# Where the last two thirds of a conditioning product are computed: TensorE beside attention, or VectorE beside the input projection

## The chip, the cores and the metric

One Trainium2 chip, one of its cores. The metric is the device time of one execution in microseconds (us), median of three runs. The core has five engines with instruction streams of their own: TensorE (PE in the profile; its weight loads are PEld), VectorE (DVE), ScalarE (ACT), GpSimd (POOL) and SyncE (SP), which here only issues transfers. They wait for each other through semaphores.

## The reference

A transformer step for 512 prompt tokens and 64 sample tokens (T = 576, model width D = 1024). What matters here:

```
mod = silu(c) @ w_ada + b_ada                    # c: 2 x 1024, w_ada: 1024 x 6144
sh1, sc1, gt1, sh2, sc2, gt2 = split(mod, 6)
h   = x * (1 + sc1) + sh1
z   = h @ w_in                                   # 1024 x 2112, in 17 blocks of 128 columns
cq, ckv = rms_norm(z[first 6 blocks]), rms_norm(z[next 2 blocks])
...   q = cq @ w_uq, attention over 4 heads, a gated branch, mix @ w_o
x1  = LN(alpha * x + (1 + gt1) * mix)            # gt1 needed here
h2  = x1 * (1 + sc2) + sh2                       # sc2, sh2 here
x2  = LN(alpha * x1 + (1 + gt2) * PEER(h2))      # gt2 at the very end
```

Only sh1 and sc1 are needed before the input projection. PEER, the mixture of 16384 small experts, takes the last three quarters of the time and is not touched.

## The kernel before

All activations lie transposed, channels on the 128 partitions and 576 tokens along the free axis in two halves of 288. Dense float32 products are made of three matmuls in a rounded format: `w_hi*x_hi`, `w_hi*x_lo`, `w_lo*x_hi`. For each block of 128 output columns SyncE loads 512 KB of weights into one of four slots of `w_raw` (function `stream`), ScalarE copies them to `w_hi`, then VectorE (`linear`, L1169) or GpSimd (`low_parts`, L428) subtracts to get `w_lo`; `w_hi` and `w_lo` have two buffers each. TensorE runs 48 matmuls a block, and ScalarE copies the result out of PSUM into `z` (function `out`). ScalarE's program for block b is: the high part of block b, then the copying out of block b-1.

The input projection is `w_in` (blocks 0 to 7, the low-rank q and kv) and `w_in2` (blocks 8 to 16). In `w_in` VectorE makes the low parts and, behind them, the squares of each block (`low_rank_squares`, L1188); in `w_in2` GpSimd makes the low parts. After block 8 TensorE sums the squares over the partitions with a matrix of ones (`low_rank_sums`, semaphore `rowsA`); VectorE scales the sums (L1192, L1193), ScalarE takes the roots, VectorE inverts (L1195), scales q and kv (L1198, L1202).

The product `silu(c) @ w_ada` is done on TensorE with silu(c) as the stationary operand (128 x 2) and the weights as the moving one. A "row" of `ada` is 512 KB and two matmuls of 512 columns, each of which the trace shows as two instructions. Sixteen rows give sh1 and sc1 before the projection. The other 32 rows come later: `ada2` (16 rows, one in each of the first 16 of the 20 units of attention, after `scores` and before `turned`), `ada3` (8, after attention, while the norm of the mixed heads is computed) and `ada4` (8, while LN1 is computed). A unit is one head and one tile of queries: scores, maximum (VectorE), exponential (ScalarE), norm (VectorE), transpose (TensorE, `turned`, L686), copy (ScalarE), product with the values (`values`). `new_keys` transposes a tile of new keys for output; its first one stands before the first unit, with a wait for ScalarE's copy behind it.

SyncE's queue holds the weight loads in program order; a load waits until its slot's previous block has its low part.

## Time and profile before

| | us |
|---|---|
| median of 3 runs | 2003.26 (1999.28 to 2005.17) |
| the profiled execution, own time | 2004.94 |
| its span in the profile | 2003.1 |
| granted TensorE clock, mean | 0.978 of full |

| engine | busy us | share |
|---|---|---|
| TensorE | 1912.8 | 95% |
| VectorE | 1399.2 | 70% |
| ScalarE | 744.3 | 37% |
| GpSimd | 422.1 | 21% |

Stages, from the same profile: conditioning and entry norm until 65 us, input projection 65 to 183, `w_uq`, keys and values until 257, attention 257 to 348, norm and `w_o` until 437, LN1 until 486, `w_pq` and PEER after that. The span includes all of it; a share of busy time is an average over these stages, so a change to one of them is read in its own window.

### The profile page before, as it was taken

Reading aid. Unit: us, or ns where it says so; the run is one execution under the profiler, and the core shown is the slowest. Engines: PE = TensorE matmul, PEld = TensorE weight load, DVE = VectorE, ACT = ScalarE, POOL = GpSimd, SP = SyncE. Lnnn points to the kernel's source line nnn. Section 1 sums busy time; section 2 is a strip of 40 time slices with the busy share of each in tenths; the row PEclk is TensorE's granted clock in tenths of the full one; section 3 lists DMA queues with packets and bytes.
Section 4 is the critical chain, followed back from the end, with each engine's and each line's share of the span. In section 5 each row is a group of like instructions: output and inputs, shape, how many; then the busy total and the mean of one; then the engine's idle time right before and its main releaser. Section 6 shows DMA issues by size and latency. Waiting matters only on the chain.

```text
span 2003.1 us, 27471 instructions
## 1 busy us (share of the span) xinstructions
PE 1912.8 (95%) x10275; PEld 1688.0 (84%) x10275; DVE 1399.2 (70%) x2739; ACT 744.3 (37%) x1154; POOL 422.1 (21%) x338
## 2 busy tenths in 40 slices
PE   7799999897998999999999999999999999999995
PEld 1799744685997999999999999989999999999995
DVE  3542444636887788987987998766767777777776
ACT  1223244212122333664565466623333333333332
POOL 1124100203320112221221222241222212122212
PEclk9899989998998999999999999999999999999997
DMA  8112123314223677887788788899999999999971
GB/s 282 64 64 89 43 80 107 127 43 137 66 71 107 213 217 225 296 291 255 258 298 273 238 300 297 313 370 340 319 311 311 319 313 322 311 316 313 313 246 69
DMA packets 189728, 447.16 MB, mean 223 GB/s; under 512 B 15792, under 2 KB 105920, under 8 KB 185888
## 3 DMA queue, kind: packets, MB, share of 16 engines
q1 hardware_dynamic: 150752, 304.13, 46.3%
q0 software_dynamic: 38848, 141.34, 20.1%
q8 instruction: 78, 1.28, 0.2%
q14 instruction: 50, 0.41, 0.1%
HBM read 383.46 MB, written 61.95 MB: 222 GB/s over the span
## 4 chain that ended last, share of the span: by engine, by line
PE 89%; DVE 6%; DMA 2%; ACT 1%; issue 1%; SPq 1%; POOL 1%; POOLq 0%; ACTq 0%; DVEq 0%
PE ps L492 88%; DMA w_raw<-peer_v 1%; SPq L378 1%; DMA gath<-peer_u,expert 0%; DMA consts_sb<-consts 0%; DVE tmp L1149 0%; PE ps L686 0%; DVE h2T L1149 0%; DVE rows L1310 0%; DVE x0T L1352 0%; DMA w_raw<-ada 0%; DVE stats L1576 0%; POOL act_lo L435 0%; DVE x0T L1351 0%; DVE x0T L1127 0%
## 5 line engine op out<-in xcount | busy, mean ns | idle before, releaser
L492 PE MATMUL ps<-act_hi,w_hi 128*128 128x448 f32 (+1 forms) x1752 | 603.1, 344 | 26.6 <-DVE act_lo L1158 11.9
L857 ACT ACTIVATE w_hi<-w_raw 128x1024 fp32r<-128x1024 f32 (+1 forms) x303 | 319.3, 1054 | 811.4 <-PE ps L492 798.8
L492 PE MATMUL ps<-act_hi,w_lo 128*128 128x448 f32 (+1 forms) x1752 | 592.8, 338 | 0.0
L492 PE MATMUL ps<-act_lo,w_hi 128*128 128x448 f32 (+1 forms) x1752 | 592.8, 338 | 0.0
L1396 DVE TENSOR_TENSOR w_lo<-w_raw,w_hi 128x1024 fp32r<-128x1024 f32 x256 | 313.6, 1225 | 282.4 <-ACT w_hi L857 282.0
L492 PE MATMUL ps<-ga_hi,w_hi 128*128 128x448 f32 x1024 | 374.7, 366 | 4.4 <-DVE ga_lo L1512 4.4
L492 PE MATMUL ps<-ga_hi,w_lo 128*128 128x448 f32 x1024 | 374.6, 366 | 0.0
L492 PE MATMUL ps<-ga_lo,w_hi 128*128 128x448 f32 x1024 | 374.6, 366 | 0.0
L492 PEld LDWEIGHTS ps<-act_hi,w_hi 128*128 128x128 f32 x1752 | 333.6, 190 | 43.6 <-issue 16.0
L492 PEld LDWEIGHTS ps<-act_hi,w_lo 128*128 128x128 f32 x1752 | 333.0, 190 | 15.6
L492 PEld LDWEIGHTS ps<-act_lo,w_hi 128*128 128x128 f32 x1752 | 333.5, 190 | 14.7
L480 POOL DMA_INDIRECT gath<-peer_u,expert x128 | 164.3, 1283 | 577.0 <-DVE act_v L1517 484.3
L480 POOL DMA_INDIRECT gath<-peer_v,expert x128 | 127.0, 992 | 476.1 <-DVE f_tok L1525 461.3
L492 PEld LDWEIGHTS ps<-ga_hi,w_hi 128*128 128x128 f32 x1024 | 192.7, 188 | 20.0 <-DVE w_lo L1396 4.7
L492 PEld LDWEIGHTS ps<-ga_lo,w_hi 128*128 128x128 f32 x1024 | 192.8, 188 | 15.3
L492 PEld LDWEIGHTS ps<-ga_hi,w_lo 128*128 128x128 f32 x1024 | 192.7, 188 | 15.3
L1525 DVE SCALAR_TENSOR_TENSOR f_tok<-gath,act_g,f_tok 128x1024 f32<-128x1024 f32 x128 | 163.5, 1278 | 0.5
L1517 DVE CUSTOM_DVE_ANT_0 gath<-gath,h_tok 128x1024 f32<-128x1024 f32 x128 | 154.2, 1219 | 10.8 <-DMA gath<-peer_u,expert 10.8
L428 POOL TENSOR_TENSOR w_lo<-w_raw,w_hi 128x1024 fp32r<-128x1024 f32 (+1 forms) x33 | 77.1, 2338 | 218.8 <-ACT w_hi L857 218.7
L857 ACT ACTIVATE piece<-ps 128x512 f32<-128x512 f32 x112 | 112.4, 1109 | 0.0
L492 PEld LDWEIGHTS ps<-one_i,one_j 128*128 128x128 f32 x896 | 108.8, 192 | 1.5
L492 PE MATMUL ps<-one_i,one_j 128*128 128x128 f32 x896 | 109.1, 275 | 0.0
(220 smaller groups left out, 1692.0 us busy)
## 6 DMA issues: line engine op xcount, KB each, us to landing
w_raw<-peer_uT SPq DMA_DIRECT2D x128, 512.0 KB, 4.6
w_raw<-peer_v SPq DMA_DIRECT2D x128, 512.0 KB, 5.4
early_activations<-e_out SPq DMA_DIRECT2D x128, 224.0 KB, 5.2
dense_gates<-piece SPq DMA_DIRECT2D x28, 1024.0 KB, 6.8
a_in<-early_activations SPq DMA_DIRECT2D x128, 224.0 KB, 5.7
g_in<-dense_gates SPq DMA_DIRECT2D x64, 448.0 KB, 6.7
w_raw<-ada SPq DMA_DIRECT2D x48, 512.0 KB, 3.3
w_raw<-w_in SPq DMA_DIRECT2D x17, 512.0 KB, 3.2
```

What stands on the lines that cost most here:

```text
L378: sp.dma_start(g_in[:, k % 2, sub].rearrange("p s i t -> p s (i t)"), src).then_inc(s_gi[k % 2], 16)
L428: nc.gpsimd.tensor_tensor(w_lo[:, g, 0:kk * P], w_raw[:, slot, 0:kk * P], w_hi[:, g, 0:kk * P].bitcast(F32), ALU.subtract).then_inc(s["wlo ...
L480: pool.indirect_dma_start(out=gath[:, n % GB, :], out_offset=None, in_=table, in_offset=bass.IndirectOffsetOnAxis(ap=expert[:, k:k + 1], a ...
L492: return nc.tensor.matmul(out, lhsT, rhs, start=start, stop=stop)
L857: return nc.scalar.activation(out, in_, func, **kw)
L1396: v.tensor_tensor(LO[c % 3], w_raw[:, (R0 + c) % RING], HI[c % 3].bitcast(F32), ALU.subtract).then_inc(s["wlo"], 1)
L1517: v.tensor_tensor_reduce(gath[:, n % GB], gath[:, n % GB], h2_tok[:], 1.0, 0.0, ALU.mult, ALU.add, act_v[:, n:n + 1]).then_inc(s["gd"], 1)
L1525: v.scalar_tensor_tensor(f_tok[:], gath[:, n % GB], act_g[:, k:k + 1], f_tok[:], ALU.mult, ALU.add).then_inc(s["gd"], 1)
```

## The change

The 32 later rows leave TensorE. Their weights are stored the other way round (`ada_rows`: 32 rows of 128 outputs x 1024 inputs, 512 KB each as before), and VectorE computes each as two dot products along the free axis with silu(c), which is laid out on all partitions (`silu_row`, 1 MB, a broadcast load on GpSimd's queue, then one activation). Twenty-two rows are computed during `w_in` and the first of `w_in2`, ten after the scaling of q and kv. In exchange GpSimd makes the low parts of all 17 blocks but the first too (VectorE made those of blocks 1 to 7), and ScalarE makes the squares of blocks 0 to 7, each just ahead of its copy out of PSUM. ScalarE's root of the sums stands one block later (`at={3: ...}`). The rows go through three buffers (`ada_in`), loaded by SyncE between the weight blocks; the load of row n waits until n-2 rows are computed. Attention keeps `new_keys` alone, spread over units 1, 3, 6, 8 and 11.

```diff
+NEW_AT = (1, 3, 6, 8, 11)
-ORDER = dict(ada=2 * KD, w_in=Z_KR, w_in2=Z_N - Z_KR, w_uq=6, ada2=2 * KD, ada3=KD, w_o=KD, ada4=KD, w_pq=HP)
+ORDER = dict(ada=2 * KD, w_in=Z_KR, w_in2=Z_N - Z_KR, w_uq=6, w_o=KD, w_pq=HP)
+ROWBUF = 3
+ROW_LOADS = (3, 2, 3, 2, 3, 2, 3, 2, 3, 2, 3, 2, 2)
+EARLY_ROWS = 22
...
+            def load_row(n):
+                wait(sp, s["adar"], n - ROWBUF + 1)
+                sp.dma_start(ada_in[:, n % ROWBUF], a["ada_rows"][n]).then_inc(s_ar[n % ROWBUF], 16)
...
+            for name in ("w_in", "w_in2"):
+                load = stream(name, a["w_in"][FIRST[name]:])
+                for b in range(ORDER[name]):
+                    load(b, b % RING)
+                    step_at = FIRST[name] + b - RING + 1
+                    if step_at >= 0:
+                        for n in range(rows_at, min(NROW, rows_at + (ROW_LOADS + (0, 0))[step_at])):
+                            load_row(n)
...
+            pool.dma_start(silu_row[:].rearrange("p c k -> p (c k)"), a["c_row"].partition_broadcast(P)).then_inc(s_cr, 16)
             pool.dma_start(ckvT[:, :, SEQ:NEW], a["cacheT"]).then_inc(s_cache, 16)
...
+            low_parts("w_in", 1)
             low_parts("w_in2")
...
-            new_keys(0)
-            pe.wait_ge(s["ote"], 1)
             for i, (h, t) in enumerate(units):
                 if i + 2 < len(units):
                     scores(i + 2)
-                if i % 4 == 0 and 0 < i <= ORDER["ada2"]:
-                    ada_columns(first + i // 4 - 1, ps[:, 6, 2 * i - 8:2 * i])
-                if i < ORDER["ada2"]:
-                    ada_row(first + i // 4, i % 4)
-                else:
-                    new_keys(i - ORDER["ada2"] + 1)
+                if i in NEW_AT:
+                    new_keys(NEW_AT.index(i))
...
-            for g in range(2):
-                ada_rows(ADA_AT["ada3"] // 4 + g)
...
-            for g in range(2):
-                ada_rows(ADA_AT["ada4"] // 4 + g)
...
+                        f(tmp[:, b, :].rearrange("p (s h) -> p s h", s=2), ps[:, pair:pair + 2, 0:H], ACT.Square).then_inc(s["sqz"], 1)
...
-            linear("w_in2", z[:, Z_KR:], at={2: low_rank_deviations}, then="w_uq")
+            linear("w_in2", z[:, Z_KR:], at={3: low_rank_deviations}, then="w_uq")
...
+            def mod_row(n):
+                if n == 0:
+                    dve.wait_ge(s["silur"], 1)
+                wait(dve, s["adar"], n)
+                dve.wait_ge(s_ar[n % ROWBUF], 16 * (n // ROWBUF + 1))
+                for c, out in ((0, ada_scratch[:]), (1, ada_in[:, n % ROWBUF])):
+                    ins = v.tensor_tensor_reduce(out, ada_in[:, n % ROWBUF], silu_row[:, c], 1.0, 0.0, ALU.mult, ALU.add,
+                                                 mod[:, 2 * KD + n, c:c + 1])
+                ins.then_inc(s["adar"], 1)
+
+            for n in range(EARLY_ROWS):
+                mod_row(n)
...
+            for n in range(EARLY_ROWS, NROW):
+                mod_row(n)
+            dve.wait_ge(s["adar"], NROW)
+            conditioning(2 * KD, 6 * KD)
```

How the instructions stand. First SyncE's queue in the input projection, where `w_raw<-w_in` is the load of one weight block. Before, the 17 loads follow each other:

```order
L352 DMA w_raw<-w_in 128x1024 x17
L352 DMA w_raw<-w_uq 128x768 x6
```

Of the change, from block 11's load on (`ada_in<-ada_rows` is the load of rows to be dotted; the first three rows here are rows 20 to 22):

```order
L369 DMA ada_in<-ada_rows 128x1024 x3
L363 DMA w_raw<-w_in 128x1024
L369 DMA ada_in<-ada_rows 128x1024 x2
L363 DMA w_raw<-w_in 128x1024
L369 DMA ada_in<-ada_rows 128x1024 x3
L363 DMA w_raw<-w_in 128x1024
L369 DMA ada_in<-ada_rows 128x1024 x2
```

What moved: the three weight loads here are those of blocks 12, 13 and 14, and block 14's now stands behind the loads of rows 25, 26 and 27, each of which waits for a computed row.

Second VectorE at the place where the sums of squares are taken up. Before:

```order
L1169 TENSOR_TENSOR w_lo<-w_raw,w_hi 128x1024
L1188 TENSOR_TENSOR tmp<-z 128x576 x2
L1192 TENSOR_SCALAR rows<-ps 128x576
L1193 TENSOR_SCALAR rows<-ps 128x576
L1195 RECIPROCAL rows<-rows 128x1152
L1198 SCALAR_TENSOR_TENSOR tmp<-z,vecs_sb,rows 128x576 x6
```

Of the change (an `ISA` row with `ada_in` as input is one dot product, the `mod 128x1` row behind it writes its sum):

```order
L1206 ISA ada_scratch,mod<-ada_in,silu_row 128x1024 [waits ada_row_landed0,s_adar]
L1206 ISA mod 128x1
L1206 ISA ada_in,mod<-ada_in,silu_row 128x1024
L1206 ISA mod 128x1
L1215 TENSOR_SCALAR rows<-ps 128x576 [waits s_rowsA,s_lo_odd,s_hlo]
L1216 TENSOR_SCALAR rows<-ps 128x576
L1218 RECIPROCAL rows<-rows 128x1152 [waits s_std]
```

What moved: in place of seven low parts and eight squares, 44 dot products now stand between the projection's start and L1215, and 20 more behind the scaling of kv.

## Rows read from the trace of the kernel before

**Rows 1.** The page, engines over the span and the chain that ended last

```profile
PE 1912.8 (95%) x10275; PEld 1688.0 (84%) x10275; DVE 1399.2 (70%) x2739; ACT 744.3 (37%) x1154; POOL 422.1 (21%) x338
PE 89%; DVE 6%; DMA 2%; ACT 1%; issue 1%; SPq 1%; POOL 1%; POOLq 0%; ACTq 0%; DVEq 0%
```

**Rows 2.** Windows: length; PE, PEld, DVE, ACT, POOL busy; clock, DMA share, GB/s

```profile
65.00:183.00 118.00, 118.00 (x848) 116.10 (x848) 34.88 (x31) 28.56 (x35) 26.22 (x13) 0.98 0.23 80
...
340.00:348.00 8.00, 5.52 (x36) 3.66 (x34) 2.90 (x12) 4.43 (x14) 2.73 (x6) 1.00 0.13 42
...
357.00:370.00 13.00, 12.32 (x33) 2.61 (x32) 11.62 (x7) 3.10 (x4) 0.68 (x1) 1.00 0.63 205
...
455.00:470.00 15.00, 13.47 (x35) 2.63 (x33) 14.68 (x20) 3.81 (x6) 2.38 (x2) 1.00 0.73 220
```

**Rows 3.** Window of one head of attention (five units), same columns

```profile
301.00:322.60 21.60, 21.50 (x88) 8.80 (x87) 8.86 (x34) 8.92 (x27) 0.00 (x0) 1.00 0.35 123
```

**Rows 4.** The same window, ScalarE's instructions on prob alone (the exponentials)

```profile
301.00:322.60 21.60, 5.30 (x18) 1.00 0.35 123
```

**Rows 5.** Timeline of TensorE: four rows of ada3 (start, us, engine, line, operation)

```profile
356.70 7.03 PE L492 MATMUL ps<-w_raw,silu_c 128*2 128x512 f32 x16
```

**Rows 6.** Timeline: GpSimd's low part, ready ahead of w_o's first matmul

```profile
374.59 2.85 POOL L428 TENSOR_TENSOR w_lo<-w_raw,w_hi 128x1024 fp32r<-128x1024 f32 x1
...
377.55 0.58 PE L492 MATMUL ps<-act_hi,w_hi 128*128 128x288 f32 x1 [3.93 <-issue]
```

**Rows 7.** Timeline of VectorE: dot products of 1024 elements back to back

```profile
1343.08 1.22 DVE L1517 CUSTOM_DVE_ANT_0 gath<-gath,h_tok 128x1024 f32<-128x1024 f32 x1
...
1344.22 1.22 DVE L1517 CUSTOM_DVE_ANT_0 gath<-gath,h_tok 128x1024 f32<-128x1024 f32 x1
1345.37 0.08 DVE L1517 DVE_READ_ACCUMULATOR2_ANT act_v<- 128x1 f32 x1
```

**Rows 8.** Line 1217 on VectorE, ns min/median/max of its four

```profile
L1217 DVE TENSOR_TENSOR tmp<-z x4: 743/751/2404, 194.6 to 198.2; 128x576 f32<-128x576 f32 x4
```

**Rows 9.** Timeline of VectorE and GpSimd at that place

```profile
194.56 4.42 DVE L1217 TENSOR_TENSOR tmp<-z 128x576 f32<-128x576 f32 x4
194.82 2.21 POOL L428 TENSOR_TENSOR w_lo<-w_raw,w_hi 128x768 fp32r<-128x768 f32 x1 [2.91 <-ACT w_hi L857]
```

**Rows 10.** Timeline of VectorE in the input projection

```profile
63.99 3.98 DVE L1158 TENSOR_TENSOR act_lo<-tmp,act_hi 128x576 fp32r<-128x576 f32 x4
...
132.18 0.76 DVE L1192 TENSOR_SCALAR rows<-ps 128x576 f32<-128x576 f32 x1 [12.68 <-PE ps L492]
...
146.86 3.94 DVE L1202 SCALAR_TENSOR_TENSOR ckvT<-z,vecs_sb,rows 128x512 f32<-128x512 f32 x4
```

**Rows 11.** Timeline of ScalarE and GpSimd around blocks 12 to 14

```profile
157.61 0.65 ACT L857 ACTIVATE z<-ps 128x576 f32<-128x576 f32 x1 [4.76 <-PE ps L492]
158.16 1.05 ACT L857 ACTIVATE w_hi<-w_raw 128x1024 fp32r<-128x1024 f32 x1
163.97 0.65 ACT L857 ACTIVATE z<-ps 128x576 f32<-128x576 f32 x1 [4.76 <-PE ps L492]
...
159.35 2.40 POOL L428 TENSOR_TENSOR w_lo<-w_raw,w_hi 128x1024 fp32r<-128x1024 f32 x1 [3.96 <-ACT w_hi L857]
```

**Rows 12.** The page, DMA issues: KB each, median us to landing

```profile
w_raw<-w_in SPq DMA_DIRECT2D x17, 512.0 KB, 3.2
```

**Rows 13.** Windows of 2 us at the projection's start, columns as in rows 2

```profile
66.00:68.00 2.00, 2.00 (x10) 2.00 (x10) 2.00 (x3) 0.00 (x0) 0.68 (x1) 0.50 0.00 0
68.00:70.00 2.00, 2.00 (x12) 2.00 (x11) 1.10 (x1) 0.00 (x0) 0.00 (x0) 0.67 0.00 0
...
74.00:76.00 2.00, 2.00 (x18) 2.00 (x17) 1.52 (x2) 1.13 (x2) 0.00 (x0) 1.00 0.00 0
```

**Rows 14.** The first 20 us: a piece of the chain, and the window

```profile
14.68 7.20 DMA w_raw<-ada
...
0.00:20.00 20.00, 8.90 (x16) 1.48 (x16) 6.19 (x13) 1.64 (x3) 5.38 (x13) 1.00 0.90 313
```

More of the change, by code:

```diff
@@ L127 @@
 S0 = SPLIT_AT["w_pq"] + HP
-FIRST = dict(ada=0, ada2=3 * KD, ada3=2 * KD, ada4=5 * KD, w_in=0, w_in2=Z_KR)
-ADA_AT = dict(ada=0, ada2=2 * KD, ada3=4 * KD, ada4=5 * KD)
-WIDTH = dict(ada=KD, ada2=KD, ada3=KD, ada4=KD, w_in=KD, w_in2=KD, w_uq=QK, w_o=KD, w_pq=KD)
+FIRST = dict(w_in=0, w_in2=Z_KR)
+NROW = 4 * KD
+ROWBUF = 3
+ROW_LOADS = (3, 2, 3, 2, 3, 2, 3, 2, 3, 2, 3, 2, 2)
+EARLY_ROWS = 22
+WIDTH = dict(ada=KD, w_in=KD, w_in2=KD, w_uq=QK, w_o=KD, w_pq=KD)
 def wait(eng, sem, value):
@@ L213, in build @@
         r_T = at("r_T", [P, KD, T], R["z"])
+        silu_row = at("silu_row", [P, 2, D], R["q"])
+        ada_in = at("ada_in", [P, ROWBUF, D], R["q"] + 8192)
+        ada_scratch = at("ada_scratch", [P, D], R["q"] + 8192 + ROWBUF * 4096)
+        assert R["q"] + 12288 + ROWBUF * 4096 <= R["kr"]
         h2T = at("h2T", [P, KD, T], R["z"] + KD * T * 4)
@@ L348, in load @@
                     if held.startswith("ada"):
-                        wait(sp, s["adaused"], b + (g0 - RING - RING_AT[held] + ADA_AT[held] + 1))
+                        wait(sp, s["adaused"], b + (g0 - RING - RING_AT[held] + 1))
                     else:
@@ L352, in load @@
                     sp.dma_start(w_raw[:, slot, 0:width], dram[b]).then_inc(s_w[slot], 16)
-                in_steps(sp, ORDER[name], RING, load)
-            for name in ORDER:
-                stream(name, a[name.rstrip("234")][FIRST[name]:] if name in FIRST else a[name])
+                return load
+            def load_row(n):
+                wait(sp, s["adar"], n - ROWBUF + 1)
+                sp.dma_start(ada_in[:, n % ROWBUF], a["ada_rows"][n]).then_inc(s_ar[n % ROWBUF], 16)
+            in_steps(sp, ORDER["ada"], RING, stream("ada", a["ada"]))
+            rows_at = 0
+            for name in ("w_in", "w_in2"):
[6 more added lines that the diff above has]
+                            load_row(n)
+                        rows_at += ROW_LOADS[step_at] if step_at < len(ROW_LOADS) else 0
+            for n in range(rows_at, NROW):
+                load_row(n)
+            for name in ("w_uq", "w_o", "w_pq"):
+                in_steps(sp, ORDER[name], RING, stream(name, a[name]))
             def load_block(c):
@@ L495, in ada_row @@
             def ada_row(g, j):
[L497 to L498 removed]
+                r = 4 * g + j
                 if j == 0:
@@ L702, in _ @@
             pe.wait_ge(s["vte"], NT)
-            first = ORDER["ada"] // 4
             scores(0)
@@ L911, in out @@
                     func = ACT.Gelu_apprx_tanh if name == "w_in2" and b > 0 else ACT.Copy
-                    f(to.rearrange("p (s h) -> p s h", s=2), ps[:, pair:pair + 2, 0:H], func).then_inc(s["evac"], 1)
-                in_steps(act, ORDER[name], RING, one)
+                    if name == "w_in":
+                        if b == 0:
+                            act.wait_ge(s["hlo"], KD // 2)
+                            act.wait_ge(s["lo_odd"], ODD["cq"])
+                        f(tmp[:, b, :].rearrange("p (s h) -> p s h", s=2), ps[:, pair:pair + 2, 0:H], ACT.Square).then_inc(s["sqz"], 1)
+                    f(to.rearrange("p (s h) -> p s h", s=2), ps[:, pair:pair + 2, 0:H], func).then_inc(s["evac"], 1)
+                if name == "w_in":
+                    for b in range(ORDER[name]):
+                        one(b, b % RING)
+                else:
+                    in_steps(act, ORDER[name], RING, one)
                 if callable(then):
@@ L987, in _ @@
                 ins.then_inc(s["pte"], 1)
-                if i % 4 == 0 and 0 < i <= ORDER["ada2"]:
-                    ada_copy(ORDER["ada"] // 4 + i // 4 - 1)
                 if 2 <= i < 2 + GH:
                     gated_squares(i - 2)
-                if i > ORDER["ada2"]:
-                    new_keys(i - ORDER["ada2"])
                 if i >= NT + 2 and (i - 2) % NT == 0:
                     head_squares((i - 2) // NT - 1)
-            new_keys(NT - 1)
             head_squares(HEADS - 1)
@@ L1000, in _ @@
             f(rows[:, 0:2], rows[:, 0:2], ACT.Sqrt).then_inc(s["std"], 1)
-            ada_copy(ADA_AT["ada3"] // 4)
             act.wait_ge(s["nv"], 16)
@@ L1006, in _ @@
                 if k == 3:
-                    ada_copy(ADA_AT["ada3"] // 4 + 1)
                     first_high("w_o")
@@ L1181, in row @@
                 return rows[:, i].rearrange("p (s h) -> p s h", s=2)
[L1183 to L1189 removed]
+            def mod_row(n):
[9 more added lines that the diff above has]
+                mod_row(n)
+            dve.wait_ge(s["hlo"], KD // 2)
+            dve.wait_ge(s["lo_odd"], ODD["cq"])
             dve.wait_ge(s["rowsA"], 1)
```

47 lines of the change are left out of this document (16 added, 31 removed).

## The prediction

> **What bounds the kernel now.** I read the page first: TensorE is busy 95% of the span and holds 89% of the chain that ended last [rows 1]. The change touches only the first 490 us, so the average says little; next come the windows by stage, and the question in each is whether TensorE waits. In the input projection it does not: 118.00 busy us in 118 [rows 2], while VectorE works 34.88 and GpSimd 26.22. In attention one head takes 21.60 us, of which TensorE is busy 21.50 [rows 3]: there too TensorE is the bound. In the two windows that hold `ada3` and `ada4` it is busy as well (12.32 of 13, 13.47 of 15), but beside it VectorE is busy 11.62 and 14.68 with a reciprocal and with LN1 [rows 2], and those are what the next product waits for. So the change takes work from TensorE where TensorE is the bound (attention) and where it is not (the two norms), and adds work to VectorE where VectorE has slack. What has to be read is whether the slack is there when it is wanted.
>
> **Removed: `ada2`.** Four rows one behind the other take 7.03 us [rows 5], 1.76 a row. A head of five units carries five, 8.8 us; TensorE alone would need 21.5 - 8.8 = 12.7 us a head. Then another loop binds, in which each step waits for the one before: exponential (ScalarE), norm, copy and next maximum (all VectorE). Its work in the window is ScalarE's 5.30 [rows 4] and VectorE's 8.86 [rows 3], 14.2 us; with some 20 hand-overs and two or three places where ScalarE's copy or square is longer than VectorE's maximum I take 16.3. Saved: 5.3 us a head, and the rows lie in 16 of 20 units, 3.2 heads: **17.0 us**. Ends: 13 (TensorE's own order holds up two units of each head) and 20.
>
> **Removed: `ada3`, `ada4`.** Worth nothing. `w_o`'s first matmul, at 377.55, follows GpSimd's low part, which ran from 374.59 to 377.44 [rows 6], and this hangs on the heads' norm, not on TensorE. `ada4` ends before LN1 does [rows 2]. Bounds: 0 to 1 us gained (ScalarE loses four small copies). Both products start at half clock today after idle time and will again.
>
> **Added at the start: the broadcast.** 1 MB is put on GpSimd's queue ahead of the cached keys. DMA is at 90%, 313 GB/s, in the first 20 us, and TensorE's chain waits 7.20 us for an `ada` load there [rows 14]. At 313 GB/s, 1 MB is 3.3 us; the load shares rather than queues behind it. Between 0 and 3.3 I take **+2.0**. The activation over 2048 elements on ScalarE falls into idle time while VectorE fills `tmp`.
>
> **Moved in the input projection.** This is the large term. I follow one path.
>
> First the port. Of four equal element-wise operations at L1217 three took 0.75 us and one 2.404 [rows 8]; GpSimd's low part ran from 194.82 to 197.03 [rows 9], and the long one is exactly the remainder of that plus its own 0.75. So an operation of VectorE with two inputs in SBUF stood still while GpSimd subtracted. The dot products have two inputs in SBUF as well; no row shows one beside a GpSimd operation. I take them to stand still too, for 2.40 us a block [rows 11]; the other end is that they run on.
> The Trainium skill, "SBUF — State Buffer", section "Who interferes with whom", says that a VectorE instruction with two SBUF inputs and a GpSimd instruction that reads SBUF exclude each other for the whole instruction. By that rule the dots are blocked; by plain sharing of the time the stage would lose less, as in the first rival.
>
> A row of two dots: 1343.08 to 1345.45 is 2.37 [rows 7], with a semaphore 2.42. VectorE starts on them when `act_lo` is done, 67.97 [rows 10]; now GpSimd's low part of block 1 comes in between, 70.4. TensorE's first block waits for the same `act_lo`, which I keep in the sum by measuring from 70.4. Twenty-two rows are 53.2 us, and the low parts of about ten blocks fall among them, 24.0: done at 147.6. The sums of squares were taken up at 132.18 [rows 10], so they are now 15.4 late. From there to the end of the scaling it took until 150.80 [rows 10], 18.6 us; again 18.6 gives 166.2. (ScalarE sits in front of the root meanwhile, and TensorE's block 12 comes some 4 us late; this is swallowed by what follows.)
>
> Then SyncE. Block 14's load stands behind the load of row 27, which waits for 25 rows computed: three more, 7.3 us, so 173.5. The load lands 3.2 later [rows 12], 176.7; high part 1.05, a dot in flight about 0.6, low part 2.40 [rows 11]: TensorE starts block 14 at 180.8. Before, block 13's result was fetched at 163.97 [rows 11], so block 14 started there: **16.8 us late**. Blocks 15 and 16 come just in time behind it. After such a gap TensorE restarts at half clock: 10 matmuls in 2 us against 18 [rows 13]; at the projection's start this lasted until about 69.3, some 4.4 us from its first matmul, a loss of **1.9**. Sum of the stage: **+18.7**.
>
> What is queued behind: ScalarE's copies out wait behind the high part; VectorE's last rows end near 198, before TensorE ends the stage (183 + 18.7), so `w_uq` isn't held up further. GpSimd's low part takes twice VectorE's time, but it is ready before the block ends: copy and square 1.3, high part 1.05, wait at most 1.2, low part 2.40, together 6.0 of a block of 6.36 (163.97 - 157.61, rows 11). Moving squares and low parts therefore costs nothing by itself; without that cover it is the third rival. `low_rank_squares` on VectorE was never on the path.
> Ends of this term: 10.1 if the dots are not blocked (below), 23 if each row costs 2.6.
>
> **Sum.** 2004.94 (profiled execution, own time) + 18.7 + 2.0 - 17.0 = 2008.6, that is +3.7; on the median of 2003.26, which lies 1.7 below the profiled one, **2007**. Two large terms of opposite sign nearly cancel. What this kernel's measurement can tell from no change is about 0.3%, 6 us.
>
> **Rivals.**
> (1) *The dots run beside GpSimd.* For: nothing in the trace shows this operation blocked. Against: [rows 8, 9]. Then 22 rows end near 122, before the sums; the root waits for ScalarE's new place behind block 11 and is some 7.5 us later than now, the scaling ends at 158, block 14's load goes at 165.4, TensorE starts it at 172.2: 8.2 + 1.9 = 10.1 for the stage. 2007 - 8.6 = 1998, from there to 1994 if attention gives 20.
> (2) *TensorE's clock stays low in attention (slower).* With 12.7 us of work in 16.3 TensorE is busy 78%. At half clock its 12.7 become nearly 25, and attention is then no shorter than today's 21.6. Against: in 340 to 348, units that already carry no `ada`, it was busy 5.52 of 8 us and the clock stayed at 1.00 [rows 2]. It decides if the half clock, which attention starts with, lasts for more than a head and a half; lost half of the time it leaves 5 of the 17 us: 2019.
> The Trainium skill, "TensorE: Matmul & The Clock Gate", section "HAM oscillation — how this bites in real kernels", tells of a kernel whose waits between tiles throttle the clock again each time. By that rule the gaps of a unit would have to be long; here they are 1 to 2 us, so the trace and the rule leave this a small chance.
> (3) *GpSimd's low parts are late in every block.* If a request waits for both dots of a row, 2.3 us, the low part is ready after 7.05 us of 6.36, 0.7 us a block over 15 blocks: some 10 us before the big gap, part of it swallowed: 2013 to 2019. It decides from a wait of 1.6 us on.
>
> **Chances.** Forecast (stage +14 to +23, attention -14 to -19, total 2001 to 2013) 0.58; rival (1) 0.22; (2) 0.12; (3) 0.08. Within 0.3% is 1997.3 to 2009.3: of the forecast two thirds, of (1) 0.6, of (3) little: 0.50. Faster by more: a third of (1) and a tail of the forecast where attention gives 20 and the broadcast nothing, together 0.15. Slower: a third of the forecast's lower gains, (2) and (3): 0.35. The forecast's own range is 2001 to 2013; the range that leaves out no more than 2 in 10 is 1996 to 2018.
>
> **What the new profile would show.** Right: a gap of TensorE of 10 us or more ahead of block 14, with SyncE's load of it behind `ada_in` loads; dots of which some last 3.6 us instead of 1.2, those beside a GpSimd low part; sums taken up on VectorE near 147; a head of attention in 16 to 17 us at clock 1.00; no change of length between attention's end and `w_pq`. Wrong: dots all at 1.2 us, block 14 on time, or windows of attention at 0.5. Most likely to upset the number are the size of the gap and the rate of a head; each us of the one is worth a us of the end.

## The result, and the profile after

The changed kernel takes 2013.73 us (median of 20 runs, 2007.54 to 2028.59), the kernel before in the same comparison 2004.95 (20 runs, 1999.17 to 2021.69). The ratio is 1.0049, 95% interval 1.0029 to 1.0069: slower by half a per cent, 5.8 to 13.8 us. The totals of one kernel fall into two groups (the kernel before, in the 100 runs of all comparisons here: 50 from 1999 to 2008 us, 50 from 2011 to 2022), and the mix differs between comparisons, so a median below is to be read by its ratio, not against another comparison's median: the kernel before had 2012.7 us beside the runs whose names begin with a, 2015.4 beside b and 2011.5 beside c. The forecast was 2007, range 1996 to 2018, and its likeliest case "within 0.3%". The range held the time; the case that came, slower by more than 0.3%, had a chance of 0.35. The execution profiled took 2022.12 us (span 2020.3). The page's engines, and its chain by engine and by line:

```profile
PE 1877.5 (93%) x10115; PEld 1685.2 (83%) x10115; DVE 1485.9 (74%) x2849; ACT 751.3 (37%) x1158; POOL 446.0 (22%) x346
...
PE 82%; DVE 10%; issue 2%; DMA 2%; ACT 1%; SPq 1%; POOL 1%; POOLq 0%; DVEq 0%; ACTq 0%
PE ps L523 81%; DVE ada_in L1206 1%; DVE ada_scratch L1206 1%; DMA w_raw<-peer_v 1%; ACT prob L871 1%; SPq L407 1%; POOL act_lo L464 0%; DMA w_raw<-ada 0%; DMA gath<-peer_u,expert 0%; DMA consts_sb<-consts 0%; DVE h2T L1165 0%; DVE tmp L1165 0%; PE ps L716 0%; DVE tmp L1341 0%; DVE rows L1336 0%
```

Against [rows 1], TensorE lost 35 us of work and VectorE took on 87, and TensorE's share of the chain fell from 89 to 82%: a part of the chain now runs over the dots (L1206). TensorE did get rid of its work; the time went elsewhere.

**Where.** Total times of one kernel differ by 15 us and more from run to run, so I cut each profile at five marks: the first low part of the modulated input (VectorE), the statistics of the gated values (VectorE, `rows<-ps` behind the input projections), the first row maximum of attention, the row statistics behind attention (356.8 us before, where [rows 5] begin), and the first gather of `peer_u`. The columns are the lengths between the starts of these, in us: the projections, the stretch to attention, attention, and from there to the gather. All thirteen profiles are in it; what each kernel is stands with its experiment.

```
profile                         start  project.  to att.  attention  to gather | gather at
before                           64.0   126.2     67.1     99.5       323.0    | 679.8
after                            66.3   141.6     67.2     85.5       324.1    | 684.7
b4_after_again (same kernel)     67.0   141.9     67.1     88.1       324.0    | 688.1
a1_loads_behind                  66.4   137.1     66.4     89.8       324.0    | 683.7
a3_filler                        64.9   144.0     67.1     88.3       322.2    | 686.5
b3_low_on_vector                 66.3   139.0     67.2     84.7       324.2    | 681.4
a2_no_ada2                       63.6   125.9     67.1     83.7       321.5    | 661.8
c2_no_ada34                      62.4   126.5     67.2     99.7       325.9    | 681.7
c3_broadcast_only                66.8   126.1     67.1     99.4       323.9    | 683.3
a4_sixteen                       64.3   129.0     67.1     89.9       322.3    | 672.6
b1_late_broadcast                64.3   127.2     67.1     85.7       322.5    | 666.8
b2_small_filler                  66.6   127.2     67.1     83.2       322.0    | 666.1
c1_combined                      68.1   127.0     67.1     85.8       321.0    | 669.0
```

So at 680 us the change costs 4.9 us in one profile and 8.3 in the other: the start +2.3 and +3.0, the projections +15.4 and +15.7, attention -14.0 and -11.4, the stretch behind it +1.1 and +1.0 (its cause is in experiment 8).

**The projections.** VectorE's timeline of the changed kernel, and GpSimd's beside it (start in us, length in us):

```profile
66.32 6.15 DVE L1174 TENSOR_TENSOR act_lo<-tmp,act_hi 128x576 fp32r<-128x576 f32 x4
72.40 1.21 DVE L1206 CUSTOM_DVE_ANT_0 ada_scratch<-ada_in,silu_row 128x1024 f32<-128x1024 f32 x1
73.54 0.08 DVE L1206 DVE_READ_ACCUMULATOR2_ANT mod<- 128x1 f32 x1
73.54 1.22 DVE L1206 CUSTOM_DVE_ANT_0 ada_in<-ada_in,silu_row 128x1024 f32<-128x1024 f32 x1
...
79.63 3.29 DVE L1206 CUSTOM_DVE_ANT_0 ada_scratch<-ada_in,silu_row 128x1024 f32<-128x1024 f32 x1
...
92.14 3.42 DVE L1206 CUSTOM_DVE_ANT_0 ada_in<-ada_in,silu_row 128x1024 f32<-128x1024 f32 x1
```

```profile
79.11 2.72 POOL L457 TENSOR_TENSOR w_lo<-w_raw,w_hi 128x1024 fp32r<-128x1024 f32 x1 [7.25 <-ACT w_hi L871]
...
91.84 2.64 POOL L457 TENSOR_TENSOR w_lo<-w_raw,w_hi 128x1024 fp32r<-128x1024 f32 x1 [3.13 <-ACT w_hi L871]
```

A dot alone lasts 1.22 us; the two beside a low part of GpSimd last 3.29 and 3.42: they end 1.1 us after the low part does, so they stood still until it was done. This is the blocking that the prediction took over from [rows 8, 9] to an operation that no row showed. (By the rule of the Trainium skill's page "SBUF — State Buffer", "Who interferes with whom", that the prediction cites, it had to be so; the trace agrees.)

Now the chain that ended last, in the stretch around block 14 (start, length, what):

```profile
169.92 0.33 SPq L369
170.25 0.04 issue
170.29 5.42 DMA w_raw<-w_in
175.73 1.07 ACT w_hi L871
176.84 0.09 issue
176.93 2.40 POOL w_lo L457
179.33 0.04 issue
179.37 21.39 PE ps L523 x144
```

The load of block 14 leaves at 170.29, right behind SP's issue of a row's load (L369). ScalarE had taken block 12's result at 160.91, and block 13 takes TensorE 6.3 us more; then it stands idle for 12.2 us, its only long wait here:

```profile
PE ps L523 <- POOL w_lo L457: 12.2, 1, 12.2
```

Block 14 starts at 179.37. Measured from the start of the stage that is 13.1 us later than in the kernel before. The last three blocks take 21.4 us, 2.3 more than 3 x 6.36. The order of the queue suggests itself as the cause; experiment 1 tests it.

**Attention.** TensorE's transposes of the fourth unit of a head, one head apart, and windows of the same trace (columns as in [rows 2]):

```profile
311.19 0.66 PE L716 MATMUL ps<-consts_sb,prob 128*128 128x128 f32 x4 [1.85 <-DVE prob L1313]
...
327.14 1.07 PE L716 MATMUL ps<-consts_sb,prob 128*128 128x128 f32 x4 [1.85 <-DVE prob L1313]
```

```profile
281.00:303.00 22.00, 20.19 (x69) 11.38 (x69) 9.16 (x35) 10.56 (x32) 2.17 (x4) 0.72 0.05 15
303.00:327.00 24.00, 18.72 (x88) 10.11 (x87) 13.61 (x48) 13.69 (x39) 3.21 (x6) 1.00 0.06 18
327.00:333.00 6.00, 5.73 (x29) 4.61 (x29) 2.86 (x13) 2.45 (x9) 0.00 (x0) 0.72 0.00 0
333.00:343.00 10.00, 7.70 (x30) 3.65 (x30) 5.46 (x19) 5.61 (x16) 0.00 (x0) 1.00 0.00 0
343.00:354.00 11.00, 9.36 (x34) 7.80 (x35) 2.84 (x11) 3.59 (x8) 0.00 (x0) 0.56 0.01 1
```

A head at full clock takes 15.95 us, against 21.60 in [rows 3] and 16.3 forecast. But of these windows the granted clock is 1.00 only in those from 303 to 327 and from 333 to 343; in the others it is a mixture of 1.0 and 0.5 (2.4 and 1.2 GHz). TensorE's waits are short: 2.9 us once, at the start of attention, and none above 1.9 us after it. Before, once the clock had risen at about 272, it stood at 1.00 to the end of attention.

What the half clock costs a head is seen in `a1_loads_behind` (experiment 1), whose attention is the same program. The same transposes, one head apart:

```profile
287.51 0.66 PE L716 MATMUL ps<-consts_sb,prob 128*128 128x128 f32 x4 [1.78 <-DVE prob L1313]
...
310.35 0.66 PE L716 MATMUL ps<-consts_sb,prob 128*128 128x128 f32 x4 [0.68 <-DVE prob L1313]
...
326.29 1.12 PE L716 MATMUL ps<-consts_sb,prob 128*128 128x128 f32 x4 [1.85 <-DVE prob L1313]
```

The first of these two heads ran at a granted clock of 0.5 from 291 to 309 and took 22.84 us; the second, at 1.00 for all but its end, 15.94.

### The profile page after: what moved, and what is told of

Read it like the earlier page. It is cut to its first block, busy times and chain, and to the rows that moved or that the text cites. A ratio compares the mean times of both kernels' runs of the same rounds, so it can differ in the third digit from the quotient of the medians.

```text
span 2020.3 us, 27245 instructions
## 1 busy us (share of the span) xinstructions
PE 1877.5 (93%) x10115; PEld 1685.2 (83%) x10115; DVE 1485.9 (74%) x2849; ACT 751.3 (37%) x1158; POOL 446.0 (22%) x346
## 4 chain that ended last, share of the span: by engine, by line
PE 82%; DVE 10%; issue 2%; DMA 2%; ACT 1%; SPq 1%; POOL 1%; POOLq 0%; DVEq 0%; ACTq 0%
PE ps L523 81%; DVE ada_in L1206 1%; DVE ada_scratch L1206 1%; DMA w_raw<-peer_v 1%; ACT prob L871 1%; SPq L407 1%; POOL act_lo L464 0%; DMA w_raw<-ada 0%; DMA gath<-peer_u,expert 0%; DMA consts_sb<-consts 0%; DVE h2T L1165 0%; DVE tmp L1165 0%; PE ps L716 0%; DVE tmp L1341 0%; DVE rows L1336 0%
## 5 line engine op out<-in xcount | busy, mean ns | idle before, releaser
L457 POOL TENSOR_TENSOR w_lo<-w_raw,w_hi 128x1024 fp32r<-128x1024 f32 (+1 forms) x40 | 101.3, 2532 | 217.4 <-ACT w_hi L871 217.4
```

What stands on the lines that cost most here:

```text
L457: nc.gpsimd.tensor_tensor(w_lo[:, g, 0:kk * P], w_raw[:, slot, 0:kk * P], w_hi[:, g, 0:kk * P].bitcast(F32), ALU.subtract).then_inc(s["wlo ...
```

## The experiments

**1. The order of SP's queue.** In the changed kernel rows 25 to 27 stand ahead of block 14's load.

```diff
-ROW_LOADS = (3, 2, 3, 2, 3, 2, 3, 2, 3, 2, 3, 2, 2)
+ROW_LOADS = (3, 2, 3, 2, 3, 2, 3, 2, 3, 2, 0, 0, 0)
```

> The changed kernel with the loads of rows 25 to 31 issued behind the load of block 16, nothing else. Theory 1 (SP's queue): in the changed kernel block 14's load stood behind row 27's, was issued at 170.3 and TensorE began block 14 at 179.4, 18.5 us after block 13. Now it is issued before 150 and block 14 begins at 161 to 164, the last block of the stage leaves at 183 to 187 instead of 200.8. The ten late rows still end near 190.8 on VectorE, so the latent's low parts come at 193 to 195 instead of 202.0 and the whole program is 7 to 9 us shorter than the changed kernel, about level with the kernel before. Rival (VectorE alone sets the stage): block 14 comes early, but the low parts still start at 201 to 203, and the time is that of the changed kernel.

Measured: 2014.94 us (12 runs), ratio to before 1.0009 (0.9979 to 1.0039). ScalarE took block 12's result at 160.97 and those of blocks 13, 14 and 15 came in step, every 6.36 us (timeline of ScalarE):

```profile
160.97 0.65 ACT L871 ACTIVATE z<-ps 128x576 f32<-128x576 f32 x1 [4.76 <-PE ps L523]
...
167.33 0.65 ACT L871 ACTIVATE z<-ps 128x576 f32<-128x576 f32 x1 [4.76 <-PE ps L523]
...
180.05 0.65 ACT L871 ACTIVATE z<-ps 128x576 f32<-128x576 f32 x1 [4.76 <-PE ps L523]
192.76 0.84 ACT L871 ACTIVATE w_hi<-w_raw 128x768 fp32r<-128x768 f32 x1 [12.07 <-DMA w_raw<-w_uq]
193.51 0.63 ACT L871 ACTIVATE z<-ps 128x576 f32<-128x576 f32 x1
```

The gap ahead of block 14 is gone, so its cause is shown. Only 4.5 us of the stage came back, not 7 to 9: the same wait stands one product further on. The first load of `w_uq` now leaves behind row 31's, at 186.28 instead of 182.44; ScalarE waits 12.07 us for it with block 16's result behind it in its order, and TensorE waits 7.8 us for ScalarE. VectorE's rows ended at 194.1 instead of 190.9, because three of their dots instead of two stood still beside a low part and one row came 1.0 us late. Neither theory had this right: the queue was the cause of the gap, but with the queue mended VectorE's rows and the rows' loads set the stage.

**2. Attention without `ada2`.** The kernel before, cut (here its core; the conditioning of the second norm is a copy of the first):

```diff
-ORDER = dict(..., w_uq=6, ada2=2 * KD, ada3=KD, w_o=KD, ada4=KD, w_pq=HP)
+ORDER = dict(..., w_uq=6, ada3=KD, w_o=KD, ada4=KD, w_pq=HP)
-                if i < ORDER["ada2"]:
-                    ada_row(first + i // 4, i % 4)
-            conditioning(3 * KD, 5 * KD, ps[:, 6, 0:4 * KD], KD)
+            v.tensor_copy(mod[:, 3 * KD:5 * KD], mod[:, 0:2 * KD]).then_inc(s["mod"], 1)
```

> The kernel before without the 16 blocks of ada2 and their transposes in attention; the four loads' worth of each head are gone too, and the third and fourth sixth of the conditioning is a copy of the first two, so the output is not the reference's. The new keys are placed as in the changed kernel. No row, no broadcast. Theory 1 (TensorE's clock): attention gives back 13 to 15 us only, because the granted clock falls to half in several stretches of it; the program is about 1990 to 1992. Rival A (the prediction's step 1, 21.6 to 16.3 us a head): 17 us, about 1987 to 1988, with the clock at full in attention. Rival B: TensorE's busy time in attention was mostly idle waiting in disguise, less than 8 us.

Measured: 1988.67 us (6 runs), ratio 0.9897 (0.9862 to 0.9932). Attention took 83.7 us, 15.8 less than before: between theory 1 (13 to 15) and rival A (17). In this profile the clock was at 1.00 from 273 to 321 us, three heads of four, and at 0.50 again from 326 to 331; one profile could not yet tell the two apart.

**3. More work for TensorE in attention, to hold the clock.** In the changed kernel, in each unit ahead of `turned(i + 1)`:

```diff
+                mm(ps[0:2, 6, :], silu_c[:, 0, :], consts[:, 0:512], True, True)
```

> The changed kernel with one matmul of 2 by 512 columns more in each of the 20 attention units, onto a PSUM bank that nothing reads. Theory 1 (clock): the granted clock stays at full in attention; attention, which took 13.9 us less than before, now takes 16 to 17 us less, and the row statistics behind it begin at about 357.5 to 359 instead of 360.6; the program gains 2 to 3 us. Rival (the added work lies on the chain of scores, exponential and values): each unit becomes longer by up to the 0.9 us of the matmul, attention loses up to 18 us and the gain of the changed kernel there is gone.

Measured: 2023.0 us (12 runs), ratio 1.0037 (1.0009 to 1.0065). Both theories came true in part: the clock stood at 1.00 from 288 us to the end of attention, and a head took 18.65 us (295.57 to 314.22) instead of 15.95. Attention is 88.3 us long: what the clock gave, the longer units took. Later, in `b2_small_filler`, the version with 16 rows (below) got 192 columns instead of 512:

```diff
+                mm(ps[0:2, 6, 0:192], silu_c[:, 0, :], consts[:, 0:192], True, True)
```

> The version with 16 rows, with a matmul of 2 by 192 columns more in each of the 20 attention units, where TensorE waits for VectorE's normalised probabilities. Nothing reads it. In the version without it, attention (first row maximum to the row statistics behind it) took 89.9 us with five stretches of half clock, in the kernel without ada2 83.7 us, in the changed kernel 85.5 us. Theory 1 (the clock costs what attention lacks to 17 us): the clock stays at full and attention takes 83 to 85 us, 5 us less than without the filler. Rival A: 0.3 us a unit is not enough, the clock still falls and attention takes 85 to 91 us. Rival B: it is enough, but lies on the chain as the 512 columns did (88.3 us).

Measured: 1993.02 us (7 runs), ratio 0.9920 (0.9889 to 0.9951); attention 83.2 us, the shortest of all, as theory 1 said, but the clock did not stay at full: it fell near 280 and near 331. A head at full clock took 15.96 us (314.04 to 330.00): 192 columns lie wholly in the wait. The window over the whole of attention in four kernels without `ada2` there, one row each (`a4_sixteen`, `b4_after_again`, `after`, `b2_small_filler`); the clock is the third number from the right:

```profile
260.40:350.30 89.90, 74.97 (x280) 45.20 (x281) 39.70 (x138) 37.63 (x110) 5.39 (x10) 0.77 0.03 9
```

```profile
276.00:364.10 88.10, 74.12 (x280) 44.82 (x279) 39.51 (x138) 37.90 (x110) 5.39 (x10) 0.79 0.03 9
```

```profile
275.10:360.60 85.50, 69.80 (x279) 42.87 (x279) 39.39 (x138) 37.92 (x110) 5.39 (x10) 0.84 0.03 9
```

```profile
260.90:344.10 83.20, 72.87 (x321) 40.35 (x321) 39.44 (x139) 37.83 (x110) 5.39 (x10) 0.90 0.03 10
```

VectorE and ScalarE do the same work in all four (39.4 to 39.7, 37.6 to 37.9 us). The length follows the clock: over the seven profiles with no filler it goes 83.7 (0.88), 84.7 (0.86), 85.5 (0.84), 85.7 (0.82), 88.1 (0.79), 89.9 (0.77), 89.8 (0.75). The two profiles of one and the same changed kernel differ by 2.6 us. With `c1_combined` (0.86, 85.8) even the small filler did not hold it: there the half clock of the beginning lasted 18 us. That the small filler raises the clock is shown beyond these profiles by the mean clock over the whole span, which every run has: 0.975 to 0.978 in the seven runs of `b2_small_filler`, 0.968 to 0.974 in the eight of `a4_sixteen`, the same kernel without it (0.965 to 0.976, median 0.971, in the twelve of `b1_late_broadcast`, also without). That it also shortens the total is not shown: the intervals of the two ratios (0.9889 to 0.9951, and 0.9904 to 0.9983) overlap.

**4. Half the rows.** VectorE computes the 16 rows of `ada2` alone; `ada3` and `ada4` stay on TensorE where they stood.

```diff
-NROW = 4 * KD
-ROW_LOADS = (3, 2, 3, 2, 3, 2, 3, 2, 3, 2, 3, 2, 2)
-EARLY_ROWS = 22
+NROW = 2 * KD
+ROW_LOADS = (3, 2, 3, 2, 3, 2, 1, 0, 0, 0, 0, 0, 0)
+EARLY_ROWS = 16
```

> VectorE computes only the 16 rows that ada2 held (all of them early), ada3 and ada4 stay on TensorE where they stood in the kernel before. Theory 1: the dots end near 72.4 + 16 x 3.27 = 125, no late rows are left, no weight load stands behind a row, and the input projections end 2 to 5 us later than before (2.3 us of it the broadcast at the start); attention gives its 14 us as in the changed kernel, and ada3 and ada4 cost nothing, because the chain there goes over VectorE. The program takes 1992 to 1996, faster than both kernels. Rival: what costs in the changed kernel is the shared port and the clock and not the late rows, then this version stays at 2002 to 2008.

Measured: 1996.79 us (8 runs), ratio 0.9944 (0.9904 to 0.9983), faster than before, if not by as much as theory 1 said. The projections lost 2.8 us instead of 15.4: theory 1. Attention gave 9.6 us and not 14: its clock (0.77) was among the lowest. The rival, that the blocked dots and the clock alone cost as much, is out, since both are still there.

**5. Who takes the low parts.** In the changed kernel VectorE takes those of blocks 1 to 7 again, with two rows behind each:

```diff
+            for b in range(1, ORDER["w_in"]):
+                ...
+                v.tensor_tensor(w_lo[:, b % 2], ...).then_inc(s["wlo"], 1)
+                mod_row(2 * b - 2)
+                mod_row(2 * b - 1)
-            low_parts("w_in", 1)
```

> The changed kernel with the low parts of input projection blocks 1 to 7 taken by VectorE again, two rows behind each; GpSimd keeps those of blocks 8 to 16. Theory 1 (the two engines share a port, so a low part on GpSimd costs VectorE about 2.2 us, more than the 1.2 us that it costs on VectorE itself): a row beside no GpSimd work takes 2.41 us, 14 rows fit into the 7 blocks, and the 22nd row ends at 138 to 145 as in the changed kernel (144.4): moving the low parts bought nothing. Rival (GpSimd takes work off VectorE): the 22nd row ends later than 150, TensorE waits for low parts in the first stage and the program is over 5 us slower than the changed kernel.

Measured: 2008.87 us (12 runs), ratio 0.9999 (0.9973 to 1.0024); the 22nd row ended at 141.6. VectorE's dots and low parts from 72 to 118 us, grouped (count, busy us, mean ns, idle before):

```profile
L1205 DVE CUSTOM_DVE_ANT_0 ada_in<-ada_in,silu_row 128x1024 f32<-128x1024 f32 x15 | 20.5, 1365 | 0.0
L1205 DVE CUSTOM_DVE_ANT_0 ada_scratch<-ada_in,silu_row 128x1024 f32<-128x1024 f32 x15 | 18.3, 1221 | 0.3
L1212 DVE TENSOR_TENSOR w_lo<-w_raw,w_hi 128x1024 fp32r<-128x1024 f32 x6 | 7.4, 1226 | 4.1 <-ACT w_hi L870 4.1
```

A low part costs VectorE 1.23 us if it does it itself, and 2.1 (3.29 less 1.22) if GpSimd does it while a dot wants to run. Three dots still stood still, beside the low parts of blocks 8 to 10, against nine before the 22nd row's end in the changed kernel. The move to GpSimd did not relieve VectorE; undoing it took 2.6 us off the projections.

**6. The same kernel again, and the second pass of the experts.** The profile after had lost another 14 us in the pass over `peer_v` (614.5 us between its first and last gather, against 600.4 before), far behind anything the change touches.

> The changed kernel once more, for the second pass of the experts (from the first gather of peer_v to the last): 614.5 us in the profiled run after, 600.4 before; in four experiments 613 (two with 32 rows) and 600 to 603 (one without rows, one with 16). Theory 1 (it differs from one execution to the next, and has nothing to do with the change): a profile with about 600 us turns up for this kernel or one of 610 or more for a kernel without 32 rows. Rival (the change itself makes the second pass slower by 14 us): again 612 to 616 here, and 600 to 603 for the versions with 16 rows. All else up to the first gather of peer_u stays within 1 us of the profile that is there: 684.7.

Measured: 2014.20 us (12 runs), ratio 1.0030 (1.0003 to 1.0058): again slower, by less. From the first to the last gather of `peer_v` it took 602.8 us, and 613.0 us in `b2_small_filler`, a version with 16 rows. Theory 1: it is not the change. Its place in the trace is the rate of TensorE. The window 1600 to 1800 of `after` and of `b4_after_again`:

```profile
1600.00:1800.00 200.00, 200.00 (x970) 181.63 (x969) 143.84 (x165) 61.06 (x80) 41.46 (x42) 1.00 0.93 308
```

```profile
1600.00:1800.00 200.00, 200.00 (x988) 185.39 (x987) 146.31 (x169) 62.60 (x82) 42.92 (x43) 1.00 0.95 315
```

TensorE never waits in either and its clock is 1.00, but it starts 970 matmuls in one and 988 in the other. Behind the mark at 680 us, then, the change costs nothing that two profiles at the same rate would show: from there to the end of the span the kernel before took 1323.3 us and this second profile of the changed one 1323.5, both at the faster rate (`after`, at the slower, 1335.6). The two spans differ by 8.5 us, and 8.3 of them lie ahead of the mark.

**7. The broadcast.** Held back in the version with 16 rows:

```diff
+            pool.wait_ge(s["adaused"], 2 * KD - 4)
             pool.dma_start(silu_row[:].rearrange("p c k -> p (c k)"), a["c_row"].partition_broadcast(P)).then_inc(s_cr, 16)
```

> The version with 16 rows (the run before it), its broadcast of the conditioning row held back until 12 of the 16 ada blocks have been used. Theory 1 (the 1 MB at the start costs its transfer time): the first low parts of VectorE start 2 to 2.3 us earlier, near 62.0 instead of 64.3, and the program gains these 2 us. Rival A: the start is not bound by the transfers, no change (0 to 0.5 us). Rival B: GpSimd's own queue now holds up the cache loads or the first low part behind the wait, and the first block starts later than before.

and alone, in the kernel before:

```diff
+            pool.dma_start(silu_row[:].rearrange("p c k -> p (c k)"), a["c_row"].partition_broadcast(P)).then_inc(s_cr, 16)
```

> The kernel before with the 1 MB broadcast of the conditioning row at the start and nothing else (nobody reads it, ScalarE only waits for it before the first high part). VectorE's first low part of the normalised input started at 64.0 and 63.6 in two kernels without it, at 64.3 to 67.0 (mean 65.9) in seven with it at the start, at 64.3 with it held back. Theory 1 (prediction: +2.0, 0 to 3.3): 65 to 67, and the group of the first 16 ada matmuls stays longer than 8 us instead of 7.0. Rival (the start differs from run to run and the broadcast costs nothing): below 64.5.

Measured: held back, 1998.61 us (12 runs), ratio 0.9939 (0.9908 to 0.9970), start at 64.3; alone, 2007.88 us (10 runs), ratio 0.9991 (0.9962 to 1.0020), start at 66.8, its first long `ada` group 8.74 us against 7.04 before. (In the chain of `c3_broadcast_only`:)

```profile
23.08 8.74 PE ps L495 x16
```

Starts without a broadcast at the beginning: 62.4, 63.6, 64.0; with it: 64.3 to 67.0, mean 66.0 over eight. It costs 2 to 3 us. Held back, theory 1's 62.0 did not come: 64.3, the same as in `a4_sixteen` with the broadcast at the start, and 68.1 in `c1_combined`, where the clock was low beside the entry's transposes (40 of them took 10.74 us). So a gain from holding it back is not shown.

**8. `ada3` and `ada4` alone.** The kernel before without them; the gates are copies of the first shift:

```diff
-ORDER = dict(..., ada2=2 * KD, ada3=KD, w_o=KD, ada4=KD, w_pq=HP)
+ORDER = dict(..., ada2=2 * KD, w_o=KD, w_pq=HP)
```

> The kernel before without ada3 and ada4 (their 16 blocks, the copies and the transposes; the last gate and the first are copies of the first sixth, so the output is not the reference's); ada2 stays in attention. The prediction's step 2 gave their removal 0 to 1 us. Profiles so far, from the row statistics behind attention to the first gather: 321.5 to 323.0 us with ada3 and ada4 (five kernels), 324.0 to 324.2 without (four kernels; with a filler in attention 322.2). Theory 1 (TensorE comes to w_o and w_pq at half clock when the blocks that it did in the wait are gone): 323.5 to 325, slower by 1 to 2 us than before. Rival (step 2 as predicted): 321.5 to 323.

Measured: 2009.44 us (10 runs), ratio 1.0006 (0.9976 to 1.0036); from attention to the gather 325.9 us, the longest of all. The ratio can't tell so little, but the marks can: 321.0 to 323.9 (mean 322.3) in the seven profiles with them, 322.2 to 325.9 (mean 324.1) in the six without. Where the time goes: `w_o`'s first matmul stands 20.7 to 20.8 us behind the last mark in all thirteen profiles, so removing `ada3` costs and gains nothing. From `h2T`'s transposes, near the start of `w_pq`, to the gather it is 189.5 us in `before`, `after` and `c2_no_ada34` alike. The whole difference lies between, where `w_pq` starts. Windows there, of `c2_no_ada34` and of before:

```profile
471.00:481.00 10.00, 5.42 (x18) 4.38 (x18) 9.79 (x14) 2.05 (x3) 3.83 (x2) 0.50 0.13 52
481.00:491.00 10.00, 6.13 (x24) 5.78 (x25) 4.03 (x7) 1.63 (x2) 6.57 (x3) 0.50 0.32 123
```

```profile
472.00:482.00 10.00, 4.41 (x22) 4.16 (x22) 9.78 (x14) 2.53 (x4) 3.73 (x2) 0.66 0.24 85
482.00:492.00 10.00, 8.48 (x45) 8.13 (x45) 5.33 (x8) 2.22 (x3) 6.36 (x3) 0.66 0.40 133
```

In both kernels `w_pq` starts at half clock. The clock rises for a while with `ada4` ahead of it (0.66 against 0.50 in the windows), but that is the smaller part. The larger one is GpSimd's last low part of `h2T`. The timelines of VectorE, GpSimd and TensorE, of `c2_no_ada34`:

```profile
482.10 2.55 DVE L1347 TENSOR_SCALAR x0T<-x0T 128x4608 f32<-128x4608 f32 x1
482.23 3.67 POOL L435 TENSOR_TENSOR act_lo<-h2T,act_hi 128x576 fp32r<-128x576 f32 x1 [4.00 <-ACT act_hi L850]
485.96 0.61 PE L492 MATMUL ps<-act_hi,w_hi 128*128 128x288 f32 x1 [2.71 <-POOL act_lo L435]
```

and of before:

```profile
483.12 1.43 POOL L435 TENSOR_TENSOR act_lo<-h2T,act_hi 128x576 fp32r<-128x576 f32 x1 [4.00 <-ACT act_hi L857]
483.20 3.78 DVE L1360 TENSOR_SCALAR x0T<-x0T 128x4608 f32<-128x4608 f32 x1
484.61 0.61 PE L492 MATMUL ps<-act_hi,w_hi 128*128 128x288 f32 x1 [0.47 <-POOL act_lo L435]
```

Before, two short instructions that finish `ada4`'s gate stood in VectorE's program just ahead of the scaling of `x0T`; GpSimd came first, took 1.43 us, and the scaling waited. Here one short copy stands in their place (nothing at all in the changed kernel), the scaling comes first by 0.13 us, and GpSimd stands still until it is done: 3.67 us, and TensorE waits 2.71 for it instead of 0.47. That is 2.2 of the 2.9 us between the two profiles; from that wait's end to the transposes, where only the clock differs, it is 6.3 us against 5.7. The wait is 2.6 to 2.7 us in all six profiles without `ada4`, the changed kernel's among them, and 0.5 to 0.9 in the seven with it. Theory 1 had the time about right (325.9, where it said 323.5 to 325) and its cause wrong in the main.

**9. All together.** 16 rows, low parts of blocks 1 to 7 on VectorE, the broadcast held back, the small filler; its edits are those of 4, 5, 7 and the second of 3, one upon the other.

> The version with 16 rows, with the three things that the runs before it showed to help or not to hurt: low parts of blocks 1 to 7 on VectorE with two rows behind each, the broadcast held back until 12 ada blocks are used, and the filler of 2 by 192 columns in each attention unit. Theory 1: the three gains lie in different stages and add up: the start 2 us, the first projection stage 1 to 3 us, attention at 83 to 84 us instead of 86 to 90. The first gather of peer_u starts at 662 to 666 (before 679.8, sixteen rows 672.6, with the filler 666.1) and the program takes 1988 to 1992, 0.990 to 0.993 of before. Rival (they take from one another: what is won at the start and in the projections is waited for at the gated branch, whose chain goes over VectorE): 1993 or more, as with the filler alone.

Measured: 1996.56 us (8 runs), ratio 0.9919 (0.9888 to 0.9951), as good as `b2_small_filler` (0.9920) and no better: a miss for theory 1, with the gather at 669.0. Its start (68.1) and its attention (85.8) were both hit by the clock in the profile (mean clock 0.973, the lowest of its eight runs; the others 0.977 to 0.981); the projections took 127.0, like `b1` and `b2` before it, so the low parts on VectorE bought nothing once the rows were 16. Both beat the kernel before; beside the changed one they stand 1 per cent lower in ratio.

## Why the prediction was right or wrong

**The sum.** It gave +3.7 us. The marks give +4.9 and +8.3, the runs +5.8 to +13.8. The picture was right: two large terms that nearly cancel, no gain left. But its likeliest case, within 0.3%, did not come, and that the sum came so near was partly luck: attention gave 3 to 6 us less than forecast and the projections cost 3 us less.

**`ada2`, -17.0 us.** It measured -14.0 and -11.4. The step as put ("a head in 16.3 us") was right and even cautious: 15.95 at full clock. The step that failed is that every head would run at this rate, and with it the weight of rival (2): the prediction read "in 340 to 348 the clock stayed at 1.00" [rows 2] as evidence for 80 us, from 8 us that stood right behind full load. In all seven profiles without `ada2` and without filler the clock fell to half again after it had risen, and a head at half clock took 22.84 us. Rival (2) thus happened in part, with 3 to 6 us instead of 12. (The prediction set it aside because the kernel in "TensorE: Matmul & The Clock Gate" of the Trainium skill, section "HAM oscillation — how this bites in real kernels", has long waits and this one short ones. Here the clock fell again although, after one of 2.9 us at the start of attention, no wait was longer than 1.9 us, so the measurement goes beyond the page's case.)

**The input projections, +18.7 us.** +15.4 and +15.7. The mechanism came as written: dots blocked, sums taken up late, row 27's load ahead of block 14's, half clock after the gap. The term that was mis-sized is block 14's lateness, 13.1 us where the prediction had 16.8. By its parts: 22 rows and the low parts were put at 77.2 us (53.2 + 24.0) and took 72.0 (72.40 to 144.41), as nine low parts hit a dot at 2.1 each; from there to the end of the scaling 18.3 (18.6 forecast); the load landed 5.42 after its issue instead of 3.2, with the DMA engines 80% busy from 170 to 176 (that the rows' loads beside it are the reason is likely, not tested); the restart at half clock cost 2.3 (1.9). Block 12, said to come some 4 us late, was 1.0 late in the stage.

**The broadcast, +2.0 us.** +2.3 and +3.0; alone +2.8.

**`ada3` and `ada4`, 0 us.** Right for `ada3`, wrong in sign for `ada4`: about +1 for the stretch, and +2.9 in `c2_no_ada34`. The sentence "both products start at half clock today after idle time and will again" held. The step that failed is that nothing else hangs on `ada4`: the two short instructions on VectorE that finish its gate were what let GpSimd's last low part go ahead of the scaling of `x0T`, and without them TensorE waits 2.63 us there in the changed kernel instead of 0.47 (experiment 8). It is the same blocking as in the projections, the other way round, in a place where the prediction did not look for it. The stretch as a whole lost only 1.1 us, because the 32 column sums ahead of LN1 ran less at half clock, 9.7 us instead of 11.0 (8.0 in `a3_filler`, at 1.00 throughout, whose stretch is the shortest of the six without `ada4`).

**Low parts to GpSimd, squares to ScalarE, 0 us.** Right for TensorE: between the first block's start and 160 us it waited for no low part, and the block's period stayed at 6.36 us. Rival (3) did not occur.

**Rival (1)**, dots beside GpSimd undisturbed: refuted by the first rows shown. The medians differ by 8.8 us and the spans of the two profiles at the same rate by 8.5; experiment 6 leaves nothing of it behind the mark at 680 us. What stays open is why the second pass has two rates.

## What to carry to other kernels

SyncE issues its loads in the program's order: before a load that waits for a computation is put on it, list what stands behind it; mending one such place here moved the wait to the next product. Work taken off TensorE where it was the bound can also take away what held its clock, so count a part of the gain (here 3 to 6 of 17 us) as lost. Where VectorE and GpSimd block each other, ask of every instruction that you remove or move which of the two now comes first: two short instructions gone cost TensorE 2.2 us. And move only the part that gains: 16 of the 32 rows carried the whole gain, the other 16 cost 12 to 15 us in the projections and about two behind attention.

## What the runs showed of the hardware

- With the granted clock at 1.00 and no wait, TensorE ran the second pass at one of two rates, 969 or 970 matmuls in the 200 us from 1600, or 988 or 989, in all thirteen profiles: 613 to 614.5 us against 600 to 604 from the first gather of `peer_v` to the last. The lower rate was in four of them (one of the changed kernel's two, two variants with 32 rows, one with 16); the cause is open.
- With waits of at most 1.9 us ahead of it, TensorE's clock fell to half inside attention, and where it fell differs from one execution of the same kernel to the next (mean clock 0.84 and 0.79 over the changed kernel's attention). Once it was low beside the entry's transposes (0.57 from 40 to 72 us in `c1_combined`, 0.79 in the kernel before).
- A dot of two SBUF inputs stood still while GpSimd subtracted: it lasted 3.28 to 3.42 us against 1.22. The one that starts first goes first: a low part of GpSimd, 2.40 in [rows 11], took 2.6 to 3.3 beside the dots.
- A VectorE scaling with one SBUF input (`x0T`, 4608 elements) and a GpSimd subtraction blocked each other in the same way: 2.55 and 3.67 us where the scaling came first, 3.78 and 1.43 where the subtraction did.
